# Moving four elementwise products and two scalings in a hybrid decoder kernel

## The reference

```
xn   = rmsnorm(h, norm_g);  proj = xn @ w_in
qkv  = silu(causal_depthwise_conv(proj[..., :3072], conv_w))     # 4 taps
z    = proj[..., 3072:4096]
q, k = l2norm of the heads' q, k;  g = decay logits, beta = gates
# per head and chunk, gcum = cumsum(g)
a_low = strict lower part of beta * (k k^T) * exp(gcum_i - gcum_j)
u, w  = solve (I + a_low) [u, w] = [v * beta, k * beta * exp(gcum)]
q_dec = q * exp(gcum);  k_dec = k * exp(gcum_last - gcum)
v_new = u - w @ S
o     = q_dec @ S + (q k^T * exp(...)) @ v_new
S     = S * exp(gcum_last) + k_dec^T @ v_new
out   = (rmsnorm(o, o_norm) * silu(z)) @ w_out
```

## Time and profile before

| | |
|---|---|
| median of three runs | 2970.71 us |
| the profiled execution | 2978.79 us |
| its span, first to last instruction | 2977.0 us |
| TensorE matmuls busy | 2580.0 us, 87% |
| VectorE busy | 1584.0 us, 53% |
| ScalarE busy | 1122.4 us, 38% |
| GpSimd busy | 595.0 us, 20% |
| projection matmuls, L1184 | 852.6 + 617.1 us |
| mean granted clock of TensorE | 0.938 |

### The profile page before, as it was taken

How to read it: one execution, slowest core, us unless ns; L and a number is a source line. 1 busy time by engine, 2 the same in 40 slices (tenths; PEclk the granted TensorE clock), 3 DMA queues, 4 the chain that set the end, 5 groups by cost and what they waited for, 6 DMA issues and landing times. The chain is left out here.

```text
span 2977.0 us, 51172 instructions
## 1 busy us (share of the span) xinstructions
PE 2580.0 (87%) x17497; PEld 2288.0 (77%) x17497; DVE 1584.0 (53%) x3692; ACT 1122.4 (38%) x3278; POOL 595.0 (20%) x509
## 2 busy tenths in 40 slices
PE   5478888899999999999998579999967999999996
PEld 4477777788888888888887258888845778877875
DVE  4356666676777777677766322222324444444342
ACT  4244545444444444444443323333322332223232
POOL 0143333311121111112111000000002232322221
PEclk9779999999999999999998589999987999999998
DMA  7663443534345443443441433333333121222111
GB/s 199 197 224 136 150 149 128 189 117 143 123 130 183 137 129 112 150 124 124 130 137 38 133 99 136 123 113 137 112 128 120 64 80 57 73 68 68 67 49 45
DMA packets 262583, 358.77 MB, mean 121 GB/s; under 512 B 74466, under 2 KB 183090, under 8 KB 262482
## 3 DMA queue, kind: packets, MB, share of 16 engines
q1 hardware_dynamic: 229682, 336.32, 34.4%
q10 hardware_dynamic: 32800, 21.17, 2.4%
HBM read 242.63 MB, written 114.79 MB: 120 GB/s over the span
## 5 line engine op out<-in xcount | busy, mean ns | idle before, releaser
L1184 PE MATMUL p_psp<-xg,p_whi 128*128 128x264 f32 x4096 | 852.6, 299 | 24.1 <-POOL p_wlo L1115 19.3
L1184 PEld LDWEIGHTS p_psp<-xg,p_whi 128*128 128x128 f32 x4096 | 671.8, 196 | 27.1 <-issue 25.0
L1184 PE MATMUL p_psp<-xg,p_wlo 128*128 128x264 f32 x2048 | 617.1, 301 | 0.0
L1184 PEld LDWEIGHTS p_psp<-xg,p_wlo 128*128 128x128 f32 x2048 | 400.2, 195 | 0.0
L2243 PE MATMUL p_psq<-p_wq,p_hT 128*128 128x512 f32 x768 | 216.1, 420 | 40.4 <-DVE p_wq L2184 28.0
L962 DVE SCALAR_TENSOR_TENSOR p_acc<-p_proj,p_taps,p_acc 128x528 f32<-128x528 f32 x288 | 241.2, 837 | 8.2
L1688 PE MATMUL p_psh<-p_wo,p_o 128*128 128x512 f32 (+1 forms) x816 | 199.1, 404 | 25.3 <-DVE p_wo L1658 21.6
L983 DVE TENSOR_TENSOR p_prod<-p_Xb,p_blk 32x4 f32<-32x4 f32 (+13 forms) x448 | 200.9, 448 | 5.6
L1688 PEld LDWEIGHTS p_psh<-p_wo,p_o 128*128 128x128 f32 (+1 forms) x816 | 150.5, 187 | 67.6 <-issue 20.8
L2243 PEld LDWEIGHTS p_psq<-p_wq,p_hT 128*128 128x128 f32 x768 | 140.2, 195 | 75.0 <-issue 23.9
L2243 PE MATMUL p_pso<-p_wo,p_oT 128*128 128x512 f32 x768 | 191.0, 402 | 5.1 <-DVE p_oT L2138 5.1
(11 more groups left out here) (269 smaller groups left out, 4728.3 us busy)
## 6 DMA issues: line engine op xcount, KB each, us to landing
p_whi<-w_dram SPq DMA_DIRECT2D x92, 512.0 KB, 4.1
p_wlo<-w_dram SPq DMA_DIRECT2D x92, 512.0 KB, 5.3
p_wraw<-w_a_in SPq DMA_DIRECT2D x36, 512.0 KB, 6.0
w_dram<-p_whi SPq DMA_DIRECT2D x34, 512.0 KB, 4.1
w_dram<-p_wlo SPq DMA_DIRECT2D x34, 512.0 KB, 5.2
hT_dram<-p_hT SPq DMA_DIRECT2D x32, 512.0 KB, 2.9
p_hT<-hT_dram SPq DMA_DIRECT2D x32, 512.0 KB, 4.2
xg<-xT_dram SPq DMA_DIRECT2D x6, 2112.0 KB, 13.0
```

The costliest lines, as they stand in the source:

```text
L1184: ins = nc.tensor.matmul(ps_p[half_][:, 0:HALF], (w_hi, w_lo)[i][:, f, kc * P:(kc + 1) * P], xg[:, g % 2, j, kc, half_ * HALF:(half_ + 1) ...
```

## The change

All edits are in the second stage.

- The silu product of z stands in slot 5 instead of slot 3.
- The exponential `e_r` is its own stage, `growth`, in slot 13 (it was part of `decays` in slot 11). The scaling of the keys is `grow_keys`, in slot 14 (it was in `tokK`, slot 12). The scaling of the queries is `grow_queries`, in slot 11 of the next step (it was in `tokQ`, slot 2 of the next step). The meta chunk's scalings stand in the same slots.
- The copy of the taps is a stage `conv` in slot 3 instead of at the start of the step.
- In steps with `splitting[1]` false, that is from step 8 on, VectorE makes the silu products, in each slot behind the stages and ahead of the convolution's taps. In the steps before, GpSimd makes them, now behind the slot's stages instead of ahead of them.
- The key's silu waits for `keys_grown` in place of `queries_grown`, and the query's silu waits for `queries_grown`.

```
-        SILU = {11: (0, 0), 21: (0, 1), 0: (1, 2), 3: (1, 3)}
+        SILU = {11: (0, 0), 21: (0, 1), 0: (1, 2), 5: (1, 3)}
...
+                for q in a:
+                    put(11, "grow_queries", q, 0)
...
                 for q in p:
                     put(10, "gates", q, 0)
                     put(11, "decays", q, 0)
+                    put(13, "growth", q, 0)
+                    put(14, "grow_keys", q, 0)
+                put(3, "conv", main, 0)
...
                     nc.scalar.activation(e_g[:, at, :], e_g[:, at, :], ACT.Exp).then_inc(decay_ready, 1)
+                elif stage == "growth":
                     if not zero(p.first):
                         act.wait_ge(queries_grown, p.first)
                     nc.scalar.activation(e_r[:, at, :], g_row[:, at, :], ACT.Exp).then_inc(er_ready, 1)
...
+            def silu(q, it, f, b):
+                dve.wait_ge(sig_done, 3 * (NF * it + (f + 1)))
+                if isinstance(it, int) and it == H - 1 and f == 2:
+                    dve.wait_ge(silu_done, NF * it + f)
+                first = q[0].first
+                if f in (0, 2) and not zero(first):
+                    dve.wait_ge(kq_ps, first)
+                    dve.wait_ge((keys_grown, None, queries_grown)[f], first)
+                if f == 1 and not zero(first):
+                    dve.wait_ge(v_ps, first)
+                if f == 3 and b and not zero(b[0].first):
+                    dve.wait_ge(o_g_ready, b[0].first)
+                dst = (kT, vT, qT, zT[q[0].par])[f]
+                src = acc[:, f % 2, :] if f < 3 else proj[:, 1, 3:3 + GW]
...
+                nc.vector.tensor_tensor(dst[:, P:P + TC], src[:, META:GW], sig[:, f % 2, META:GW],
+                                        ALU.mult).then_inc(silu_done, 1)
...
-                if stage == "gates":
+                if stage == "conv":
+                    head = p.item if isinstance(p.item, int) and p.item < H else p.item % H
+                    link(nc.vector.tensor_copy(taps[:], conv_w[:, bass.ds(head * 12, 12)]))
+                elif stage == "gates":
...
-                if p:
-                    head = it if isinstance(it, int) and it < H else it % H
-                    link(nc.vector.tensor_copy(taps[:], conv_w[:, bass.ds(head * 12, 12)]))
                 for slot in schedule(it, p, a, b, splitting):
                     for stage, q, index in slot.stages:
                         stage_of(stage, q, index)
+                    if not splitting[1]:
+                        for q, item, f in slot.silu:
+                            silu(q, item, f, b)
...
-                    if f == 0:
-                        pool.wait_ge(queries_grown, first)
+                    pool.wait_ge((keys_grown, None, queries_grown)[f], first)
...
-                if stage == "tokK":
+                if stage == "grow_keys":
...
-                elif stage == "tokQ":
+                elif stage == "grow_queries":
...
-                    for q, item, f in slot.silu:
-                        silu(q, item, f, b)
                     for stage, q, index in slot.stages:
                         stage_of(stage, q, index, b)
+                    if splitting[1]:
+                        for q, item, f in slot.silu:
+                            silu(q, item, f, b)
```

More of the change, by code:

```diff
@@ L964, in convolve @@
                     nc.vector.tensor_scalar(v, src, -40.0, None, ALU.max).then_inc(conv_done, 1)
+            def silu(q, it, f, b):
[12 more added lines that the diff above has]
+                src = acc[:, f % 2, :] if f < 3 else proj[:, 1, 3:3 + GW]
+                if q[0].meta:
+                    nc.vector.tensor_tensor(dst[:, 0:META], src[:, 0:META], sig[:, f % 2, 0:META], ALU.mult)
+                nc.vector.tensor_tensor(dst[:, P:P + TC], src[:, META:GW], sig[:, f % 2, META:GW],
+                                        ALU.mult).then_inc(silu_done, 1)
             def bc(v, n):
@@ L1110, in _ @@
         def _(pool):
[L1111 to L1116, removed]
             def silu(q, it, f, b):
@@ L1135, in silu, with split_low @@
                                         ALU.mult).then_inc(silu_done, 1)
+            def split_low(it, f, part):
+                cols = slice(part * D // 2, (part + 1) * D // 2)
+                pool.wait_ge(hi_ready, 2 * (NF * it + f) + (part + 1))
+                nc.gpsimd.tensor_tensor(w_lo[:, f, cols], w_raw[:, f % 2, cols], w_hi[:, f, cols].bitcast(f32),
+                                        ALU.subtract).then_inc(lo_ready, 1)
             def stage_of(stage, p, index, b):
```

## The result

The changed kernel took 2929.26 us (median of four runs, 2923.01 to 2931.77) against 2973.15 for the kernel before (median of four, 2968.01 to 2978.11): 0.9849 of its time, 95% interval 0.9824 to 0.9875, 44 us less. The forecast was 2947.

What follows compares the result with a forecast made beforehand. TensorE was taken to set the pace, idle 3.5 us a head. Terms summed to -1.2 us a head, -29 us over 24 heads, plus 5 for the first group: -24, giving 2947 us; range 2920 to 2974.

Steps and rivals of the forecast that it cites:

- rival 1: Freed engine gives more: queries' scaling falls into one-input VectorE operations, (b) vanishes; -2.1 us a head, 2921 us; chance 0.15.
- (a): Start of a step: taps' copy goes to slot 3, `p_r` and chunk 0's product come earlier; -1.6 us a head.
- (b): First state, for chunk 1: q silu ahead of the solve's rows, queries' scaling holds the next product; +0.7 us a head.
- (c): Slots 3 to 11: VectorE gains taps' copy and z silu (+1.24), idle time covers all but +0.2 us a head.
- (e): Keys' scaling at slot 14 holds the convolution's second tap some 0.4 us; +0.1 us a head, at most +0.5.
- (f): Values: v silu queued behind a convolution tap and two rows on VectorE, ends at 1125.8; +0.1 us a head.
- (d): Keys: VectorE's silu, 0.69 + 0.05 us, replaces GpSimd's 1.28 ahead of the key transposes; -0.7 us a head.
- Silu: The 96 silu products of 128x512 on VectorE: 0.69 us each, 2.8 us a head more; bounds 0.43 to 0.76.
- First group: First 8 heads: queries' scaling behind the splits lengthens convolution taps; +0.65 us a head, +5 us, bounds -3 to +12.
- The second: VectorE is the new bound: its additions eat what is released, -0.1 us a head; 2973 us, no change; chance 0.12.
- the third: Slow small operations come from their instructions' places, not GpSimd; +1.1 us a head, 3002 us, slower; chance 0.06.

Runs made afterwards that it cites:

- e12: Changed kernel plus a useless VectorE reduction of 4x512 (2.29 us) ahead of each step's first `p_r` in the later groups; 2986.38 us, one run (before 2974.18).
- e2: Kernel before with only the copy of the taps moved to slot 3, silus and scalings as before; 2954.06 us, 0.9917 of before.
- e9: Changed kernel, but in later groups GpSimd also waits for the newer item's key silu before scaling the queries; 2914.04 us, 0.9802 of before.
- e10: Changed kernel with z's silu back in slot 3, now on VectorE; 2963.22 us in one run (before 2974.18).
- e11: Changed kernel with GpSimd's added wait for the key silu in later groups, and growth and scalings in former slots in the first group; 2900.52 us, 0.9751 of before.
- e4: Changed kernel with growth and both scalings back in slots 11, 12 and 2 in all groups; 2925.51 us, 0.9817 of before.
- e1: Changed kernel with the copy of the taps back at the start of the step; 2938.31 us, 0.987 of before.
- e3: Changed kernel with the silu products on GpSimd in all groups, new slots kept; 2949.12 us, 0.9896 of before.
- e7: Changed kernel plus a useless VectorE reduction of 3x512 (1.75 us) ahead of each step's first `p_r` in the later groups; 2964.54 us, one run (before 2972.12).
- e5: Changed kernel plus a useless GpSimd 128x512 product on scratch at the value's sigmoid, from step 8 on; 2951.22 us in one run (before 2972.12).

## Why the prediction was right, and where its sizes were off

The direction, the mechanism and the three large terms held; the gain was 44 us where 24 were forecast. The measured 2929 lies 18 us under the forecast, near the lower end of the range, which had been drawn for rival 1 and not for what happened: no term of the sum was for the clock, and that the range took the result in is in part luck.

- **(a) Start of a step.** Forecast -1.6 a head, measured -1.61 in the wait (in the head of the earlier trace rows from 1.90 to 0.42, in the one ahead of it from 1.79 to nothing). But this term was mis-sized: it priced a gap of TensorE at its length. The gaps cost some 15 us more over the 23 heads through the clock, and TensorE's busy time fell by 14.2 with the change. I took the cost from one head, and it was one of the 12 without a fall; the granted clock of 0.98 in the earlier trace rows was the sign that others differ. e12 shows that the gap alone brings the falls back, e2 that the copy's move alone removes them.
- **(b) First state.** +0.7 forecast, +0.60 measured, held as described; the product held was 32x64, not 32x49. e9 shows its cause.
- **(c), (e), (f).** +0.2, +0.1 and +0.1 forecast, all 0 measured: `p_w`'s wait is 0.5 us in both lists, and none for the values or for `acc` shows. What (e) described happened (the tap of 1.09 us), but TensorE didn't wait for it. Together 9 us over the 23 heads. I think that the cover was larger than counted, since I read VectorE's idle time with its operations still held; that is argued, not shown. The two slots' delay of z, costed at 0 on its reader's side, is needed on the other side: e10 has +1.38 a head without it.
- **(d) Keys.** -0.7 forecast, -0.70 measured.
- **Silu.** 0.69 us taken, 686 to 693 ns measured:

```profile
L990 DVE TENSOR_TENSOR p_kT<-p_acc,p_sig 128x512 f32<-128x512 f32 x23 | 15.9, 692 | 13.7 <-ACT p_sig L855 13.7
```

- **First group.** +5 forecast, +5.2 in the profile. The times say more: e11 is 13.5 us below e9 for this group's slots alone. In the ten profiles that share the changed kernel's first group it takes 432.9 to 441.4 us, mean 436.9, against 427.8 before and 426.2 in e2, which has the scalings in before's slots. So some 9, within the bounds of -3 to +12; e4 and e11, with growth and scalings in their former slots, take 429.7 and 424.3. The place is the one named, as GpSimd and VectorE show beside the earlier trace rows:

```profile
467.96 3.25 POOL L1163 TENSOR_TENSOR p_wlo<-p_wraw,p_whi 128x512 fp32r<-128x512 f32 x2 [0.26 <-ACT p_whi L830]
471.17 2.63 POOL L1179 TENSOR_TENSOR p_qd<-p_qT,p_er 128x128 f32<-128x128 f32 x2
```

```profile
470.26 2.40 DVE L968 SCALAR_TENSOR_TENSOR p_acc<-p_proj,p_taps,p_acc 128x528 f32<-128x528 f32 x2
472.79 1.04 DVE L1056 TENSOR_SCALAR p_obias<-p_ssq 128x4 f32<-128x4 f32 x1
```

In 23 heads, then: forecast -1.2 x 23 = -27.6; measured -39.5 in the three waits of (a), (b) and (d), close to the 37.7 of idle time, and -14.2 in the busy time, most of it the clock: 51.9 in all. That is 24 us more than forecast, and the first group, at 9 instead of 5, took back 4 of it, which leaves the 20 between forecast and median.

The rivals: the first (the freed engine gives more, 2921 us) had the nearer time and the wrong cause, for its mark, an unstretched product at the step's start, came only with e9. The second (VectorE as the new bound) is refuted by the waits; the third by e1. By the Trainium skill's remark that moving work between these two engines might not help (Perfetto Trace Analysis, Optimizing Scalar/DVE Operations) nothing was to be gained; the silus' move alone, e3 against after, gave 16.6 us in the 23 heads.

## What to carry to other kernels

Where a short operation of VectorE reads two SBUF inputs and takes a microsecond, look for a GpSimd product that ends with it; moving that work onto VectorE can cost VectorE next to nothing (2.4 us of busy time here), and what stays on GpSimd belongs where VectorE waits anyway, held there by a wait and not by its place in a list. Price a gap of TensorE in several heads, by the busy time of equal work and the granted clock, since it can cost more than its length. An edit's parts don't add: the slots of the scalings and of z's silu were worth 17 us with the silus on GpSimd, the scalings' slots nothing with them on VectorE, and in the first group they cost time (13.5 us by e11 against e9, 3.3 in the profile of e4).

## What the runs showed of the hardware beyond this

- The hold reached a plain copy of 128x12 elements (0.91 us against 0.16) and a 128x4 operation (1.16 against 0.15): each operation shown, from 128x4 to 128x528, was lengthened by 0.1 to 0.2 us less than what was left of GpSimd's operation, whatever its size.
- TensorE's clock fell by half 0.6 to 1.5 us behind gaps of 1.76 to 1.92 us, when the engine was busy again, and in 11 of 23 equal heads; e12 gave 11 of 23 as well, e7 none.
- A GpSimd product of 128x512 whose two inputs are the same tile took 1.04 us (e5), the scalings 1.28; the silu of z, of two tiles, took 1.13 in e2 and e3, so the same tile need not be the reason.
